# The first tile behind an output norm taken in two halves of the tokens

## The chip, the cores and the metric

The kernel runs on one core of one Trainium2 chip. The metric is the device time of one execution, in microseconds; the kernel before has a median of 3034.61 us over three runs (3032.1 to 3035.51).

## What is computed

Two blocks of a small language model, one sequence of 512 tokens, width 1024, all in float32. The second block has two layers. Each adds to x the output of a mixer (compressed, selected and windowed attention beside a stick-breaking attention) and then that of a feed-forward net with a depthwise convolution, and both outputs pass a norm of their own before they are added:

```python
x = x + rms_norm_2(mixer(rms_norm_2(x, g_pre_mix)), g_post_mix)
x = x + rms_norm_2(ffn(rms_norm_2(x, g_pre_ffn)), g_post_ffn)
# rms_norm_2(y, g) = y * rsqrt(mean(y * y, over the 1024 channels) + 1e-6) * g
```

The norms with g_post_mix and g_post_ffn are the output norms. There are four of them, two in each layer: ("p", 0, "m"), ("p", 0, "f"), ("p", 1, "m") and ("p", 1, "f") in the code.

## The kernel before

All activations lie transposed: channels on the 128 partitions, the 512 tokens along the free axis, so that x is eight tiles of 128x512, `K.x(0)` to `K.x(7)`. A product with a weight matrix is made in three passes of fp32r, each of 512 columns: high weights by high x and low weights by high x (`high`, lines 473 and 476), then high weights by low x (`low`, line 480). Weights stream from HBM through a ring. ScalarE rounds each piece of 512 columns (four 128x128 blocks) to the high part (line 996), VectorE subtracts it for the low part `wl` (line 1377); four pieces of each are held. Likewise ScalarE makes `xh(j)`, x times the gain of the next norm, rounded (`prescale`, line 1003), and VectorE the remainder `xl(j)` (line 1385). The factor of a pre-norm, one number for each token, is applied to the results only, so products start before the norm's sum is known.

The engines each run a program written out by hand, in order, and meet at semaphores: `q.wait_ge(flag, event)` is the wait, `tell` names the event.

An output norm can't be postponed in this way, since x + norm(y) is needed for the next product. Its steps:

- `post` on each engine. For each tile of y that TensorE ends, ScalarE squares it out of its bank (line 1007), VectorE adds the squares up and copies y to M (line 1787).
- TensorE: `sums` (lines 570 and 575) takes the column sums over the partitions, four products with a column of ones against the squares of tiles 0 to 6 and four against those of tile 7. The result is 128 tokens by 4 in bank 2.
- VectorE: `mean_square` (line 1399), on 128x4. GpSimd: `root` (line 1990), the power -1/2, on 128x4.
- TensorE: `spread` (line 585), four products with the identity, lays the roots as a row over all partitions, in bank 3.
- VectorE: `post_feed`, for each tile j: M times the gain times bank 3 (line 1797), x plus M (line 1800), and for the tile before, the remainder xl (line 1385).
- ScalarE: `post_feed`, for each tile j: xh(j) (line 1003) and the square of x(j) for the next norm (line 1007). GpSimd adds these squares up (`add_squares`, line 2024), one 128x512 addition for each of tiles 1 to 7.
- TensorE: `group`, five output tiles in five banks side by side, for k = 0 to 7: ten high passes with xh(k), then five low passes with xl(k).

On VectorE the feeds of tiles 0 to 2 come first; then, for each k, the feed of tile k + 3 and the low parts of the weight pieces up to the third beyond those of k. The group takes 40 blocks, that is pieces 0 to 9. The block of k = 6 and the third bank is the first of piece 8.

Behind three of the output norms a group follows. Behind the last one there is a tail (line 1975 on): VectorE makes M(0) to M(7) (line 1975) and adds x(0), x(2), x(4), x(6) (line 1979) and x(7) (line 1981), GpSimd adds x(1), x(3), x(5) (line 2064), and SyncE sends the eight tiles out in order.

`K.RSB` ("rs") is a row in SBUF. For pre-norms ScalarE copies the spread roots into it (`rs_row`, line 1011); output norms read them from bank 3.

Of the kernel before, what the change touches and what calls it, by code (L numbers as in the profile page):

```python
# [16 lines left out]
S = 512  # L17
# [21 lines left out]
for _name, _n in (("ident", 128), ("ones", 128), ("tri", 128), ("neg", 128), ("rot", 128), ("blk", 2), ("mhalf", 64),  # L39
# [6 lines left out]
         "x0", "first", "x1", "x2", "x3", "x4", "gain", "cst", "vec", "pos", "dil", "ret", "out")  # L46

# [398 lines left out]
def tensor_program(e, q, K):  # L446
# [72 lines left out]
    def group(key, nk, operand, banks, hooks):  # L519

        for k in range(nk):
            oh, parts = operand[0](k), []
# [90 lines left out]
    half = [None]  # L613

    def soft(L, steps, fill, upto):
# [3 lines left out]
        for t in range(n + 3):  # L619
# [28 lines left out]
            if 0 <= t - 3 < n:  # L648
                step = steps[t - 3]
                q.wait_ge(F.act, half[0])  # L650
# [14 lines left out]
                m.then_inc(F.attn.tell(("values", L, t - 3)), 1)  # L665
                if step.done is not None:
                    half[0] = step.done
# [47 lines left out]
    half[0] = "qkrow"  # L715
    vacated[4] = []
    soft(("e", 0), even_steps(K), fill, fill_even)
    vacated[4] = [(F.act, half[0])]
# [23 lines left out]
    def ffn(f, late):  # L742
        s = ("f", f)
        turn[0] = [0, 1, 4, 5, 6, 7]
        group(("up", f, "g"), DT, xn(s), [next_bank() for _ in range(5)], {} if late else norm(s))
# [5 lines left out]
    def post(s):  # L751

        sums(s, 6 % 3, apart=7 % 3)
        spread(s, 64, 3, F.dve, ("added", s))
# [65 lines left out]
    for l in range(2):  # L820
# [11 lines left out]
        group(("n", l, "g"), DT, xn(s), [next_bank() for _ in range(5)], {} if l else norm(s))  # L832
# [68 lines left out]
        half[0] = ("kcc", l)  # L901
# [31 lines left out]
        def sb_pv(n):  # L933
# [4 lines left out]
            if kt == 3:  # L938
                q.wait_ge(F.act, half[0])
# [3 lines left out]
            if kt == 0 and kv == 1:  # L943
                half[0] = ("os", l, j)
# [14 lines left out]
        vacated[4] = [(F.act, half[0])]  # L959
# [20 lines left out]
def scalar_program(e, q, K):  # L980
# [278 lines left out]
    def post_feed(s):  # L1259
        def feed(j):  # L1260
            q.wait_ge(F.dve, ("x", s, j))
            prescale(s, j)
# [5 lines left out]
    for l in range(2):  # L1268
        s = ("n", l)
        group(("n", l, "g"), 5, post_feed(s) if l else nothing, {} if l else {3: lambda: rs_row(s)})  # L1270
# [91 lines left out]
        ffn(2 + l, True, post_feed(("f", 2 + l)))  # L1362
        post(("p", l, "f"), ("down", 2 + l))


def vector_program(e, q, K):
# [315 lines left out]
    def rotate(h, which):  # L1682
# [10 lines left out]
        for i, (half, c) in enumerate(((0, K.cosr), (1, K.sinr), (0, K.sinr), (1, K.cosr))):  # L1693
# [3 lines left out]
            e.tensor_tensor(K.tmp(i), K.bank(keys[half])[:, :], c, ALU.mult).then_inc(F.dve.tell(*events), 1)  # L1697
# [82 lines left out]
    def post(s, key, M):  # L1780
# [191 lines left out]
    q.wait_ge(F.stat, ("spread", s))  # L1972
    q.wait_ge(F.dve, ("freed", "down", 3, DT - 1))
# [10 lines left out]
def gpsimd_program(e, q, K):  # L1984
    F = K.F
    def root(s, at, width=NQ):
# [4 lines left out]
            F.pool.tell(("rsn", s)), 1)  # L1991

# [35 lines left out]
    for l in range(2):  # L2028
# [28 lines left out]
        root(("p", l, "m"), 64)  # L2057
# [3 lines left out]
        root(("p", l, "f"), 64)  # L2061
# [163 lines left out]
```

## Time and profile before

| | |
|---|---|
| median of three runs | 3034.61 us (3032.1 to 3035.51) |
| the profiled execution, its own time | 3034.25 us |
| its span, first to last instruction | 3032.5 us |
| PE busy | 2998.2 us, 99% |
| DVE busy | 1774.3 us, 59% |
| ACT busy | 1269.7 us, 42% |
| POOL busy | 146.0 us, 5% |
| mean granted TensorE clock | 0.992 |

The span is shorter than the execution's own time by 1.75 us that lie around it. Engines are named as in the profile: PE is TensorE, DVE is VectorE, ACT is ScalarE, POOL is GpSimd. "L1797" is line 1797 of the kernel before. The granted clock is 1.00 at 2.4 GHz and 0.50 at 1.2 GHz. In the chain of waits and in the timeline a row with "x8" stands for eight records; one float32 product leaves two.

### The profile page before, as it was taken

What the parts mean: (1) busy time and instruction counts of PE and PEld (TensorE: products, weight loads), DVE (VectorE), ACT (ScalarE), POOL (GpSimd) and SP (SyncE); (2) the same over time, 40 slices, a digit from 0 to 9 for tenths busy, and PEclk for the clock granted to TensorE, in tenths of its full rate; (3) what the DMA queues carried; (4) which work ended last, traced back from release to release, by engine and by line L of the source; (5) the groups of instructions that cost most, each with busy time, mean ns of one, the idle gap of its engine ahead of it and who ended that gap; (6) DMA issues with size and microseconds to landing.
All of it is one profiled execution on the core that took longest, in us unless ns stands there. A gap on an engine that the chain in (4) does not pass through costs nothing.

```text
span 3032.5 us, 37840 instructions
## 1 busy us (share of the span) xinstructions
PE 2998.2 (99%) x14648; PEld 2400.0 (79%) x14648; DVE 1774.3 (59%) x3128; ACT 1269.7 (42%) x2377; POOL 146.0 (5%) x203
## 2 busy tenths in 40 slices
PE   9999999999999999999999999999999999999998
PEld 7778888877888888888876678888787766788886
DVE  4666775345555577634465557775364655577743
ACT  4444443322333344432366545443233655355431
POOL 0000000000000000001001101000020011010000
PEclk9999999999999999999999999999999999999999
DMA  4222322222222333333211132222232111223332
GB/s 156 71 94 94 99 97 97 98 77 84 84 77 88 93 98 97 98 97 98 92 36 43 48 99 80 101 97 98 84 102 88 36 42 49 90 84 105 98 97 70
DMA packets 72035, 260.35 MB, mean 86 GB/s; under 512 B 8112, under 2 KB 8112, under 8 KB 71728
## 3 DMA queue, kind: packets, MB, share of 16 engines
q1 hardware_dynamic: 70992, 254.52, 26.3%
q10 hardware_dynamic: 864, 3.41, 0.3%
q8 instruction: 116, 1.90, 0.3%
q14 instruction: 63, 0.52, 0.1%
HBM read 255.81 MB, written 2.10 MB: 85 GB/s over the span
## 4 chain that ended last, share of the span: by engine, by line
PE 93%; DVE 4%; ACT 2%; issue 1%; DMA 0%; POOL 0%; DVEq 0%; SPq 0%; ACTq 0%
PE bank L473 25%; PE bank L476 24%; PE bank L480 24%; PE bank L550 2%; PE bank L554 2%; PE bank L551 2%; PE bank L630 2%; PE bank L662 2%; PE bank L644 1%; PE bank L793 1%; PE bank L910 1%; DVE wl L1377 1%; DVE big L1961 1%; PE bank L940 1%; ACT big L1356 1%
## 5 line engine op out<-in xcount | busy, mean ns | idle before, releaser
L1377 DVE TENSOR_TENSOR wl<-ring,wh 128x512 fp32r<-128x512 f32 (+1 forms) x946 | 648.9, 692 | 829.2 <-ACT wh L996 824.4
L473 PE MATMUL bank<-xh,wh 128*128 128x512 f32 x2464 | 989.0, 401 | 14.1 <-ACT wh L996 7.2
L476 PE MATMUL bank<-xh,wl 128*128 128x512 f32 x2464 | 966.4, 392 | 0.3 <-DVE wl L1377 0.3
L480 PE MATMUL bank<-xl,wh 128*128 128x512 f32 x2464 | 926.2, 391 | 0.0
L996 ACT ACTIVATE wh<-ring 128x512 fp32r<-128x512 f32 (+1 forms) x946 | 581.0, 622 | 814.3 <-PE bank L480 734.7
L473 PEld LDWEIGHTS bank<-xh,wh 128*128 128x128 f32 x2464 | 466.3, 189 | 148.9 <-issue 38.4
L480 PEld LDWEIGHTS bank<-xl,wh 128*128 128x128 f32 x2464 | 465.1, 189 | 99.9 <-DVE xl L1470 0.4
L476 PEld LDWEIGHTS bank<-xh,wl 128*128 128x128 f32 x2464 | 466.9, 189 | 91.7 <-DVE wl L1377 1.3
L473 PE MATMUL bank<-bigr,wh 128*128 128x512 f32 x1024 | 399.0, 390 | 0.6 <-ACT bigr L1360 0.6
L476 PE MATMUL bank<-bigr,wl 128*128 128x512 f32 x1024 | 398.5, 389 | 0.0
L480 PE MATMUL bank<-bigr,wh 128*128 128x512 f32 x1024 | 393.4, 389 | 0.0
L473 PEld LDWEIGHTS bank<-bigr,wh 128*128 128x128 f32 x1024 | 192.2, 188 | 41.3 <-ACT bigr L1360 1.4
L480 PEld LDWEIGHTS bank<-bigr,wh 128*128 128x128 f32 x1024 | 192.2, 188 | 40.6 <-DVE bigr L1965 0.9
L476 PEld LDWEIGHTS bank<-bigr,wl 128*128 128x128 f32 x1024 | 192.2, 188 | 39.9
L1173 ACT ACTIVATE tmp<-tmp,vec 128x512 f32<-128x512 f32 x136 | 104.8, 770 | 182.1 <-DVE tmp L1427 182.1
L1065 ACT ACTIVATE pp<-pp,sm 128x512 f32<-128x512 f32 (+3 forms) x160 | 88.3, 553 | 90.7 <-DVE sm L1446 90.5
L1183 ACT ACTIVATE bigr<-tmp 128x512 fp32r<-128x512 f32 x88 | 55.6, 632 | 138.5 <-DVE tmp L1633 138.5
L1427 DVE TENSOR_TENSOR big<-bank,rs 128x512 f32<-128x512 f32 x106 | 71.7, 687 | 68.5 <-PE bank L480 65.4
L1990 POOL TENSOR_TENSOR sm<-sm,cst 128x4 f32<-128x4 f32 x16 | 16.6, 1037 | 1941.1 <-DVE sm L1399 1607.0
L1427 DVE TENSOR_TENSOR tmp<-bank,rs 128x512 f32<-128x512 f32 x154 | 105.4, 684 | 6.0 <-ACT rs L1011 4.3
L550 PE MATMUL bank<-wh,xh 128*128 128x512 f32 (+1 forms) x288 | 106.8, 371 | 0.0
L554 PE MATMUL bank<-wl,xh 128*128 128x512 f32 (+1 forms) x288 | 105.8, 367 | 0.0
(203 smaller groups left out, 2756.5 us busy)
## 6 DMA issues: line engine op xcount, KB each, us to landing
ring<-in_w_up SPq DMA_DIRECT2D x176, 512.0 KB, 3.5
ring<-in_w_down SPq DMA_DIRECT2D x88, 512.0 KB, 3.4
ring<-in_w_in SPq DMA_DIRECT2D x64, 512.0 KB, 3.5
ring<-in_w_ret SPq DMA_DIRECT2D x32, 512.0 KB, 3.3
ring<-in_w_even SPq DMA_DIRECT2D x19, 512.0 KB, 3.3
ring<-in_w_ret_v SPq DMA_DIRECT2D x16, 512.0 KB, 3.3
ring<-in_w_ret_out SPq DMA_DIRECT2D x16, 512.0 KB, 3.3
ring<-in_w_proj SPq DMA_DIRECT2D x16, 512.0 KB, 3.5
```

Of the source, the lines that this page charges most:

```text
L473: e.matmul(o, K.wh(p, c * 128, 128), oh, start=start, stop=False, skip_group_check=True)
L476: e.matmul(o, K.wl(p, c * 128, 128), oh, start=False, stop=False, skip_group_check=True)
L480: m = e.matmul(o, K.wh(p, c * 128, 128), ol, start=False, stop=stop, skip_group_check=True)
L550: e.matmul(o, K.XH[:, c], K.wh(p, 0, n), start=k == 0, stop=False)
L551: e.matmul(o, K.XL[:, c], K.wh(p, 0, n), start=False, stop=False)
L554: m = e.matmul(o, K.XH[:, c], K.wl(p, 0, n), start=False, stop=k == DT - 1)
L630: m = e.matmul(BK[i][:, u.at:u.at + w], u.q[r, u.qt * 128:w], u.k[r, 0:w], start=True, stop=True, skip_group_check=True)
L996: e.activation(K.wh(i, 0, w), K.raw(i), ACT.Copy, bias=0.0, scale=1.0).then_inc(F.hi.tell(("piece", i)), 1)
L1065: e.activation(p, p, ACT.Exp, bias=K.den(t, 2 * part + i, 0), scale=-1.0, accum_out=K.den(t, 2 * part + i, 1)).then_inc(F.act.tell(("exp", ...
L1173: e.activation(K.tmp((2 * i + 1) % 5), K.up(i), ACT.Identity, bias=b, scale=w[2]).then_inc(F.act.tell(("tap", f, i)), 1)
L1377: e.tensor_tensor(K.wl(i, 0, w), K.raw(i), K.wh(i, 0, w).bitcast(F32), ALU.subtract).then_inc(F.lo.tell(("piece", i)), 1)
L1427: e.tensor_tensor(dst, K.bank(key)[:, :], K.RSB[:, :], ALU.mult).then_inc(F.dve.tell(("freed", *key), *events), 1)
```

## The change

Each output norm is taken by halves of 256 tokens. Half 0 lies in bank 2 and half 1 in bank 3, from the sums to the spread roots. The sums, the mean squares (now two instructions of 128x2), the roots (two of 128x2) and the spreading tell an event for each half. The first tile of x is scaled, added and rounded to xh(0) in two halves, and in the group behind the norm the ten high passes of k = 0 become twenty of 256 columns: ten on half 0, then ten on half 1. ScalarE copies each half of the spread roots to `K.RSB`, behind VectorE's own reading of that half (`half_row`), and tiles 1 to 7 are scaled with `K.RSB` in SBUF where they were scaled with bank 3 in PSUM. The tail does so too, with tile 0 scaled in halves and then added whole. `half(ap, a)` is columns a * 256 to a * 256 + 255; the variable `half` of the tensor program is renamed `held`.

```diff
 tensor_program, group (called with border=True for the groups behind an output norm)
+            if border and k == 0:
+                s = ("f", key[1]) if key[0] == "up" else key[:2]
+                for a in range(2):
+                    q.wait_ge(F.act, ("xh", s, 0, a))
+                    for m, b in enumerate(banks):
+                        if a == 0:
+                            empty(b)
+                            K.place[(*key, m)] = b
+                            vacated[b] = [(F.dve, ("freed", *key, m))]
+                            parts.append(take())
+                        high(half(BK[b], a), *parts[m], half(K.xh(0), a), a == 0)
+                ol = operand[1](k)
+                for m, b in enumerate(banks):
+                    low(BK[b][:, :], *parts[m], ol, False)
+                continue
 tensor_program, post
-        sums(s, 6 % 3, apart=7 % 3)
-        spread(s, 64, 3, F.dve, ("added", s))
+        q.wait_ge(F.dve, ("sq", s))
+        empty(2)
+        empty(3)
+        for i in range(NQ):
+            e.matmul(BK[2 + i // 2][:, i:i + 1], K.tmp(6 % 3)[:, i * 128:(i + 1) * 128], K.cs("ones", 1), start=i % 2 == 0,
+                     stop=False, skip_group_check=True)
+        q.wait_ge(F.act, ("sq", s, DT - 1))
+        for i in range(NQ):
+            m = e.matmul(BK[2 + i // 2][:, i:i + 1], K.tmp(7 % 3)[:, i * 128:(i + 1) * 128], K.cs("ones", 1), start=False,
+                         stop=i % 2 == 1, skip_group_check=True)
+            if i % 2:
+                m.then_inc(F.stat.tell(("sums", s, i // 2)), 1)
+        for i in range(NQ):
+            if i % 2 == 0:
+                q.wait_ge(F.pool, ("rsn", s, i // 2))
+            m = e.matmul(BK[2 + i // 2][:, i * 128:(i + 1) * 128], bc(K.SM[:, 64 + i:65 + i], [[0, 128]]), K.cs("ident"),
+                         start=True, stop=True, skip_group_check=True)
+            if i % 2:
+                m.then_inc(F.stat.tell(("spread", s, i // 2)), 1)
+        vacated[2] = vacated[3] = [(F.act, ("rs", s))]
 scalar_program
+    def half_row(s, a):
+        q.wait_ge(F.stat, ("spread", s, a))
+        q.wait_ge(F.dve, ("m", s, 0, a))
+        e.activation(half(K.RSB, a), half(BK[2 + a], a), ACT.Copy, bias=0.0, scale=1.0).then_inc(
+            F.act.tell(("rsh", s, a), *([("rs", s)] if a else [])), 1)
 scalar_program, post_feed
-            q.wait_ge(F.dve, ("x", s, j))
-            prescale(s, j)
+            if j == 0:
+                for a in range(2):
+                    half_row(before, a)
+                    q.wait_ge(F.dve, ("x", s, 0, a))
+                    e.activation(half(K.xh(0), a), half(K.x(0), a), ACT.Copy, bias=0.0,
+                                 scale=K.vec(GAIN[s][0], GAIN[s][1])).then_inc(
+                        F.act.tell(("xh", s, 0, a), *([("xh", s, 0)] if a else [])), 1)
+            else:
+                q.wait_ge(F.dve, ("x", s, j))
+                prescale(s, j)
 vector_program, post
-        mean_square(s, DT * 128)
+        for a in range(2):
+            q.wait_ge(F.stat, ("sums", s, a))
+            e.tensor_scalar(K.SM[:, 2 * a:2 * a + 2], BK[2 + a][:, 2 * a:2 * a + 2], 1.0 / (DT * 128), EPS, ALU.mult,
+                            ALU.add).then_inc(F.dve.tell(("ms", s, a)), 1)
+    def half_scale(s, key, M, gain, a):
+        q.wait_ge(F.stat, ("spread", s, a))
+        q.wait_ge(F.dve, ("freed", *key, DT - 1))
+        e.scalar_tensor_tensor(out=half(M[0], a), in0=half(M[0], a), scalar=gain, in1=half(BK[2 + a], a), op0=ALU.mult,
+                               op1=ALU.mult).then_inc(F.dve.tell(("m", s, 0, a), *([("m", s, 0)] if a else [])), 1)
 vector_program, post_feed
-            q.wait_ge(F.stat, ("spread", s))
             if j == 0:
-                q.wait_ge(F.dve, ("freed", *key, DT - 1))
-            e.scalar_tensor_tensor(out=M[j], in0=M[j], scalar=K.vec(gain, gi + j), in1=BK[3][:, :], op0=ALU.mult,
-                                   op1=ALU.mult).then_inc(F.dve.tell(("m", s, j), *([("added", s)] if j == DT - 1 else [])), 1)
-            q.wait_ge(F.dve, ("m", s, j))
-            e.tensor_tensor(K.x(j), K.x(j), M[j], ALU.add).then_inc(F.dve.tell(("x", nxt, j)), 1)
+                for a in range(2):
+                    half_scale(s, key, M, K.vec(gain, gi), a)
+                    q.wait_ge(F.dve, ("m", s, 0, a))
+                    e.tensor_tensor(half(K.x(0), a), half(K.x(0), a), half(M[0], a), ALU.add).then_inc(
+                        F.dve.tell(("x", nxt, 0, a)), 1)
+            else:
+                q.wait_ge(F.act, ("rs", s))
+                e.scalar_tensor_tensor(out=M[j], in0=M[j], scalar=K.vec(gain, gi + j), in1=K.RSB[:, :], op0=ALU.mult,
+                                       op1=ALU.mult).then_inc(F.dve.tell(("m", s, j)), 1)
+                q.wait_ge(F.dve, ("m", s, j))
+                e.tensor_tensor(K.x(j), K.x(j), M[j], ALU.add).then_inc(F.dve.tell(("x", nxt, j)), 1)
 vector_program, the tail behind the last output norm
     for j in range(DT):
-        e.scalar_tensor_tensor(out=XM[j], in0=XM[j], scalar=K.vec("g_post_ffn_2", 8 + j), in1=BK[3][:, :], op0=ALU.mult,
-                               op1=ALU.mult).then_inc(F.dve.tell(("m", s, j)), 1)
+        if j == 0:
+            for a in range(2):
+                half_scale(s, ("down", 3), XM, K.vec("g_post_ffn_2", 8), a)
+        else:
+            q.wait_ge(F.act, ("rs", s))
+            e.scalar_tensor_tensor(out=XM[j], in0=XM[j], scalar=K.vec("g_post_ffn_2", 8 + j), in1=K.RSB[:, :], op0=ALU.mult,
+                                   op1=ALU.mult).then_inc(F.dve.tell(("m", s, j)), 1)
 gpsimd_program
+    def half_roots(s):
+        for a in range(2):
+            q.wait_ge(F.dve, ("ms", s, a))
+            e.tensor_tensor(K.SM[:, 64 + 2 * a:66 + 2 * a], K.SM[:, 2 * a:2 * a + 2], K.cs("mhalf", 2), ALU.pow).then_inc(
+                F.pool.tell(("rsn", s, a)), 1)
```

## Rows read from the trace of the kernel before

**Rows 1.** Page, part 4: the chain that ended last, share of the span by engine

```profile
PE 93%; DVE 4%; ACT 2%; issue 1%; DMA 0%; POOL 0%; DVEq 0%; SPq 0%; ACTq 0%
```

**Rows 2.** Chain of waits after the output norm at 1816 us: start us, us, what

```profile
1817.21 0.97 PE bank L575 x8
1818.20 0.17 DVE sm L1399
1818.44 1.02 POOL sm L1990
1819.51 1.17 PE bank L585 x8
1820.70 0.76 DVE big L1797
1821.48 0.70 DVE x L1800
1822.21 0.73 ACT xh L1003
1822.98 0.79 PE bank L473
```

**Rows 3.** The spreading in the chain at the third and the fourth output norm

```profile
2647.04 2.09 PE bank L585 x8
3019.49 2.09 PE bank L585 x8
```

**Rows 4.** Stretches: length, busy of PE, PEld, DVE, ACT, POOL, granted clock, DMA, GB/s

```profile
1822.98:1852.63 29.65, 29.65 (x121) 24.37 (x122) 24.14 (x31) 15.07 (x25) 10.02 (x7) 0.92 0.26 88
2194.08:2224.21 30.13, 30.13 (x121) 24.71 (x122) 24.39 (x31) 14.85 (x25) 9.81 (x7) 0.91 0.30 87
2651.43:2681.55 30.12, 30.12 (x121) 24.70 (x122) 24.39 (x31) 14.92 (x25) 9.82 (x7) 0.91 0.28 84
```

**Rows 5.** Chain of waits: full products at each clock, a product of 256 columns

```profile
1823.77 0.43 PE bank L476
1829.06 0.23 PE bank L476
1638.22 0.12 PE bank L927
```

**Rows 6.** Groups by form, small shapes: busy us, mean ns of one, idle before

```profile
L1997 POOL TENSOR_TENSOR sm<-sm,cst 128x64 f32<-128x64 f32 x1 | 10.6, 10642 | 41.6 <-DVE sm L1522 41.6
L1941 DVE TENSOR_TENSOR tmpr<-pp,bigr 128x256 fp32r<-128x256 f32 x16 | 6.0, 418 | 0.0
```

**Rows 7.** Timeline: start us, us, engine; VectorE and GpSimd in the first group

```profile
1824.91 1.83 POOL L2024 TENSOR_TENSOR tmp<-tmp 128x512 f32<-128x512 f32 x1 [5.46 <-ACT tmp L1007]
1825.52 1.77 DVE L1385 SCALAR_TENSOR_TENSOR xl<-x,vec,xh 128x512 fp32r<-128x512 f32 x1
...
1833.76 0.73 DVE L1797 SCALAR_TENSOR_TENSOR big<-big,vec,bank 128x512 f32<-128x512 f32 x1
1834.53 1.25 DVE L1800 TENSOR_TENSOR x<-x,big 128x512 f32<-128x512 f32 x1
1835.70 0.74 DVE L1385 SCALAR_TENSOR_TENSOR xl<-x,vec,xh 128x512 fp32r<-128x512 f32 x1
1833.93 1.30 POOL L2024 TENSOR_TENSOR tmp<-tmp 128x512 f32<-128x512 f32 x1 [1.91 <-ACT tmp L1007]
```

**Rows 8.** The late weight remainders (timeline), and their product (chain of waits)

```profile
1844.19 2.99 DVE L1377 TENSOR_TENSOR wl<-ring,wh 128x512 fp32r<-128x512 f32 x3
...
1846.97 0.23 PE bank L476
```

**Rows 9.** Timeline of the tail, VectorE and GpSimd

```profile
3021.61 1.41 DVE L1975 SCALAR_TENSOR_TENSOR xm<-xm,vec,bank 128x512 f32<-128x512 f32 x2 [3.25 <-PE bank L585]
3029.29 0.68 DVE L1981 TENSOR_TENSOR x<-x,xm 128x512 f32<-128x512 f32 x1
3023.09 1.65 POOL L2064 TENSOR_TENSOR x<-x,xm 128x512 f32<-128x512 f32 x1 [3.65 <-DVE xm L1975]
```

More of the change, by code:

```diff
@@ L46, with half @@
          "x0", "first", "x1", "x2", "x3", "x4", "gain", "cst", "vec", "pos", "dil", "ret", "out")
+def half(ap, a):
+    return ap[:, a * S // 2:(a + 1) * S // 2]
 class Flag:
@@ L517, in tile, with group @@
             pass
-    def group(key, nk, operand, banks, hooks):
+    def group(key, nk, operand, banks, hooks, border=False):
         for k in range(nk):
-            oh, parts = operand[0](k), []
+            parts = []
+            if border and k == 0:
[13 more added lines that the diff above has]
+                continue
+            oh = operand[0](k)
             for m, b in enumerate(banks):
@@ L611, in fills @@
         return fill
-    half = [None]
+    held = [None]
     def soft(L, steps, fill, upto):
@@ L649, in soft @@
                 step = steps[t - 3]
-                q.wait_ge(F.act, half[0])
+                q.wait_ge(F.act, held[0])
                 if step.cmp is not None:
@@ L666, in soft @@
                 if step.done is not None:
-                    half[0] = step.done
+                    held[0] = step.done
     def cmp_turn(l, j):
@@ L712, in tensor_program @@
         vacated[b] = [(F.dve, ("qk", j))]
-    half[0] = "qkrow"
+    held[0] = "qkrow"
     vacated[4] = []
     soft(("e", 0), even_steps(K), fill, fill_even)
-    vacated[4] = [(F.act, half[0])]
+    vacated[4] = [(F.act, held[0])]
     def mixed(k):
@@ L744, in ffn @@
         turn[0] = [0, 1, 4, 5, 6, 7]
-        group(("up", f, "g"), DT, xn(s), [next_bank() for _ in range(5)], {} if late else norm(s))
+        group(("up", f, "g"), DT, xn(s), [next_bank() for _ in range(5)], {} if late else norm(s), late)
         for i in range(5, 2 * FT):
@@ L831, in tensor_program @@
         turn[0] = [0, 1, 4, 5, 6, 7]
-        group(("n", l, "g"), DT, xn(s), [next_bank() for _ in range(5)], {} if l else norm(s))
+        group(("n", l, "g"), DT, xn(s), [next_bank() for _ in range(5)], {} if l else norm(s), l == 1)
         tile(("n", l, 5), DT, xn(s), F.dve, norm(s, 0, 4) if l else {})
@@ L900, in tensor_program @@
         fill = fills(steps(("gm", l, j), DT, xn(s), F.dve) for j in range(16))
-        half[0] = ("kcc", l)
+        held[0] = ("kcc", l)
         soft(("n", l), nsa_steps(K, l), fill, fill_nsa)
@@ L938, in sb_pv @@
             if kt == 3:
-                q.wait_ge(F.act, half[0])
+                q.wait_ge(F.act, held[0])
             e.matmul(BK[4][base:base + 64, kt * 128:S], K.SBV[:, kt * S + h * 64:kt * S + (h + 1) * 64],
@@ L943, in sb_pv @@
             if kt == 0 and kv == 1:
-                half[0] = ("os", l, j)
+                held[0] = ("os", l, j)
         for t in range(16 + 2):
@@ L958, in tensor_program @@
         fill(10 ** 6)
-        vacated[4] = [(F.act, half[0])]
+        vacated[4] = [(F.act, held[0])]
         def merged(k):
@@ L1257, in post, with post_feed @@
             square(s, j, K.bank((*key, j))[:, :])
-    def post_feed(s):
-        def feed(j):
-            q.wait_ge(F.dve, ("x", s, j))
-            prescale(s, j)
+    def half_row(s, a):
[3 more added lines that the diff above has]
+            F.act.tell(("rsh", s, a), *([("rs", s)] if a else [])), 1)
+    def post_feed(s, before):
+        def feed(j):
+            if j == 0:
[8 more added lines that the diff above has]
+                prescale(s, j)
             if j >= 3:
@@ L1269, in scalar_program @@
         s = ("n", l)
-        group(("n", l, "g"), 5, post_feed(s) if l else nothing, {} if l else {3: lambda: rs_row(s)})
+        group(("n", l, "g"), 5, post_feed(s, ("p", 0, "f")) if l else nothing,
+              {} if l else {3: lambda: rs_row(s)})
         if l:
@@ L1361, in scalar_program @@
         post(("p", l, "m"), ("wo", l))
-        ffn(2 + l, True, post_feed(("f", 2 + l)))
+        ffn(2 + l, True, post_feed(("f", 2 + l), ("p", l, "m")))
         post(("p", l, "f"), ("down", 2 + l))
+    for a in range(2):
+        half_row(("p", 1, "f"), a)
 def vector_program(e, q, K):
@@ L1692, in rotate @@
                 q.wait_ge(F.act, ("oh", 4 * h - 5))
-        for i, (half, c) in enumerate(((0, K.cosr), (1, K.sinr), (0, K.sinr), (1, K.cosr))):
+        for i, (part, c) in enumerate(((0, K.cosr), (1, K.sinr), (0, K.sinr), (1, K.cosr))):
             events = [("rt", h, which, i)]
@@ L1696, in rotate @@
                 events += [("freed", *key) for key in keys]
-            e.tensor_tensor(K.tmp(i), K.bank(keys[half])[:, :], c, ALU.mult).then_inc(F.dve.tell(*events), 1)
+            e.tensor_tensor(K.tmp(i), K.bank(keys[part])[:, :], c, ALU.mult).then_inc(F.dve.tell(*events), 1)
     def centre(h):
@@ L1971, in vector_program @@
     s = ("p", 1, "f")
-    q.wait_ge(F.stat, ("spread", s))
-    q.wait_ge(F.dve, ("freed", "down", 3, DT - 1))
     for j in range(DT):
-        e.scalar_tensor_tensor(out=XM[j], in0=XM[j], scalar=K.vec("g_post_ffn_2", 8 + j), in1=BK[3][:, :], op0=ALU.mult,
-                               op1=ALU.mult).then_inc(F.dve.tell(("m", s, j)), 1)
+        if j == 0:
[5 more added lines that the diff above has]
+                                   op1=ALU.mult).then_inc(F.dve.tell(("m", s, j)), 1)
         if j % 2:
@@ L1991, in root @@
             F.pool.tell(("rsn", s)), 1)
+    def half_roots(s):
+        for a in range(2):
+            q.wait_ge(F.dve, ("ms", s, a))
+            e.tensor_tensor(K.SM[:, 64 + 2 * a:66 + 2 * a], K.SM[:, 2 * a:2 * a + 2], K.cs("mhalf", 2), ALU.pow).then_inc(
+                F.pool.tell(("rsn", s, a)), 1)
     s = ("e",)
@@ L2056, in gpsimd_program @@
                                     channel_multiplier=-1).then_inc(F.pool.tell(("w", l, n)), 1)
-        root(("p", l, "m"), 64)
+        half_roots(("p", l, "m"))
         for j in range(DT):
@@ L2060, in gpsimd_program @@
         root(("f", 2 + l), 224)
-        root(("p", l, "f"), 64)
+        half_roots(("p", l, "f"))
     for j in (1, 3, 5):
```

## The prediction

> **What bounds the kernel now.** I read the page's chain first: TensorE holds 93% of it, VectorE 4%, ScalarE 2% [rows 1]. So only two things count, the places where TensorE stands still and the stretches in which its clock is low. The output norms are such places. The chain of waits in the window of the first one shows a relay with one engine working at a time [rows 2]: last sums 0.97, mean 0.17, root 1.02, spreading 1.17, scaling 0.76, addition 0.70, xh(0) 0.73, then the first product at 1822.98. From 1817.21 that is 5.77 us without a product of weights. The second norm has the same relay. At the third and the fourth the spreading takes 2.09 [rows 3], 0.92 more, because the clock is already at its lower level (1.2 GHz).
>
> The clock stays low behind the gap. A product of 512 columns takes 0.43 there and 0.23 at full clock [rows 5]. From restart to the end of the group the mean granted clock is 0.92, 0.91 and 0.91 [rows 4]; at two levels, 1.00 and 0.50, that is 2 x 0.08 x 29.65 = 4.7 us low, then 5.4 and 5.4.
>
> Then I looked at what feeds the group. In the timeline one feed of VectorE is scaling (L1797), addition (L1800), remainder (L1385) and one weight remainder (L1377). An operation starts 0.07 to 0.08 before the one ahead of it has ended: two scalings take 1.41 in all [rows 9], so 0.67 each from start to start, and an addition 0.61. The four would be 0.67 + 0.61 + 0.67 + 0.61 = 2.55, but the addition takes 1.25, because GpSimd began its own addition (1.30) at 1833.93 [rows 7]. So a feed costs about 3.2 against 15 x 0.227 = 3.4 of TensorE for one k. VectorE keeps ahead, but narrowly: the first of three late weight remainders, piece 8, ends at 1844.19 + 2.99 - 2 x 0.61 = 1845.96, and the product that needs it starts at 1846.97 [rows 8]. The lead is 1.0 us.
>
> **The relay by halves.** Times are of the first norm. Half 0 of the sums is done after four of eight records, 0.48 sooner, at 1817.70; VectorE's copy of the last tile stands in front of the mean, so I take 1817.75, and 1817.99 for the start of the root. GpSimd's power takes 1.02 on four columns [rows 2] and 10.64 on 64 [rows 6], 0.16 for each column, so 0.70 on two (bounds 0.51, half, and 1.02, nothing gained). Half 0 has its roots at 1818.69, half 1 at 1819.39. Spreading one half is half of 1.17: half 0 is out at 1819.31, half 1 at 1820.02. An operation of 256 columns on VectorE takes 0.42 [rows 6], a scaling 0.05 more as at 512. VectorE then does scaling, addition, scaling, addition: 1819.34, 1819.83, 1820.17, 1820.66, and is free for tile 1 at 1821.10, where it was at 1821.48 + 0.61 = 1822.09: 1.0 us sooner. ScalarE first copies half of the row (new, some 0.37, done at 1820.20 while the addition runs), then xh(0), half 0, at 1820.27: between 0.37 and 0.73, taken as 0.50. TensorE restarts at 1820.82, 2.15 sooner (1.6 to 2.5). Half 1 is rounded at 1821.65, when the first ten short products still run until about 1823.1; there is no new wait there. Behind ScalarE's new waits stand only its own feeds of tiles 1 and 2, which VectorE feeds later anyway.
>
> Twenty products of 256 columns replace ten of 512: 0.12 against half of 0.227 [rows 5], 0.1 more in all at full clock, 0 to 0.5 at the low one. Unhindered, TensorE would be 2.0 us ahead.
>
> **What takes this back.** Tiles 1 to 7 are now scaled with a row in SBUF. The scaling beside GpSimd's addition took 0.73, undisturbed, as its row lay in a bank; an operation of the same kind with both tensors in SBUF, L1385, took 1.77 behind GpSimd's 1.83, and ended 0.55 behind it [rows 7]. So two engines take turns: an operation of VectorE with two SBUF tensors doesn't run beside GpSimd's addition, in either order. The Trainium skill, page "SBUF — State Buffer", section "SBUF: two separate sides", has this as an exclusive lock for the whole instruction between a GpSimd operation and a VectorE one with two SBUF inputs; taken alone it gives 1.29 for each of GpSimd's additions, in the groups and three times in the tail. The rows price it so: GpSimd asked 0.17 behind the start of the scaling; now it must let the scaling end, 0.50 later, and everything behind it moves by that. A feed costs 3.2 + 0.5 = 3.7, more than TensorE's 3.4. VectorE becomes the bound of the group.
>
> In place of the bank's slot a scaling of its own costs the same, 0.73 against 0.74 [rows 7]. The Trainium skill, page "VectorE: DVE Perf Modes", section on the TRN2 errata, gives 58 cycles of fixed cost from SBUF and 120 from PSUM; at 0.96 GHz that would save 0.065 for each of 28 scalings, 1.8 us in all and 3031.8 us. The trace doesn't agree, and I leave it out.
>
> Piece 8 again. VectorE starts tile 1 1.0 sooner and loses 0.5 of it while the first two additions of GpSimd are placed; the three feeds from tile 4 to tile 7 cost 0.53 more each, 1.6; and GpSimd's last addition, which stood in front of the subtraction (2.99 for three [rows 8]), comes a little later than it, so 1.0 to 1.2 is saved. Sum: -0.5 + 1.6 - 1.0 = +0.1; piece 8 is ready at 1846.1. TensorE, 2.0 ahead, would want it at 1845.0, and waits 1.1. From this product to the end of the stretch there are 1852.63 - 1846.97 = 5.66. Because of the wait a clock that rises up to 2 us later costs nothing.
>
> - Group 1 ends at 1846.1 + 5.66 = 1851.8 instead of 1852.63: -0.85.
> - Group 2: restart was 371.10 later [rows 4], so 2217.2 + 5.66 = 2222.9 instead of 2224.21: -1.35.
> - Group 3: 828.45 later, less the 0.92 of slow spreading, of which half 0 pays 0.4: 2674.0 + 5.66 = 2679.7 instead of 2681.55: -1.85.
>
> Together -4.1. Bounds: -7.0, with the feeds as cheap as before, and +1.
>
> **The tail.** Here the relay matters less, since the next row copy needs half 1. The first scaling was at 3021.61, 0.92 of slow spreading included. Now half 0 is spread at 3019.8, half 1 at 3020.9; scaling and copy end at 3021.75, and tile 1 is scaled at 3021.77 instead of 3021.61 + 0.67 = 3022.28: -0.5. But GpSimd adds three tiles, 1.65 each, beside scalings from the bank [rows 9]. Now nothing of VectorE's seven scalings and five additions can run beside them. Each addition of 1.29 stops VectorE for 1.2: +3.6 (between 0, if they run beside after all, and 3 x 1.65 = 4.9). VectorE's last addition, which ended at 3029.97, ends at about 3033.1. The outputs follow as before. Tail: +3.1. Should VectorE win each turn, GpSimd's three would be left for the end, at the same price.
>
> **Sum.** 3034.25, the profiled execution's own time, - 4.1 + 3.1 = 3033.25. That execution lies 0.36 under the median, so 3033.6 for a median. SyncE's weight loads depend on pieces used and start up to 2 us earlier or not at all; each lands in its slot well ahead, and I cost them at nothing.
>
> **Rivals.**
> - A, the scaling from SBUF does run beside GpSimd. For it: nothing but that this very operation isn't in the trace. Then groups gain 2.0, 2.0 and 2.3, the tail 0.5: 3027.8. Chance 0.07.
> - B, GpSimd is served ahead of VectorE at the end of the feeds too, so that its last addition still stands before piece 8. The place is the product of 1846.97; it decides once the remainder is written later than that. Piece 8 is then ready at 1847.3 to 1847.8, groups end +0.6, +0.1 and -0.4 or 0.5 worse, tail +3.1 to +3.6: 3038.5. For it: GpSimd was ahead there before the change (three subtractions took 2.99, undisturbed they take 1.91) [rows 8]. Chance 0.2, a quarter of it beyond 0.2%, where ScalarE's later rounding adds to it.
> - C, the lower clock lasts one stretch longer in a group, as at the third norm where it fell earlier: up to 1.7 for each beyond the cover of the wait: 3035.5. Chance 0.13.
> - My case, 0.6.
>
> A measurement of this kernel can tell 0.2%, 6.1 us, from no change. A lies just beyond it; faster gets 0.06, slower 0.07, the rest 0.87. The range reaches from most of A's side, 3029.8, to B, 3038.8.
>
> **What would show it.** Right: the relay's first product some 2.1 us sooner; rows of L1797's successor with a mean well over 0.74 and up to 1.9; a wait of TensorE of 0.5 to 1.7 on wl at k = 6 in each group; the tail's VectorE stretched by 3 to 4 us. Wrong: scalings at 0.74 beside GpSimd (A), no wait on wl while the groups end 2 us sooner, or waits of over 2 us in several k.

## The result, and the profile of the changed kernel

The changed kernel takes 3038.77 us (median of 20 runs, 3032.91 to 3040.84), the kernel before 3033.65 beside it (20 runs, 3029.07 to 3035.93). The ratio is 1.0016, 95% interval 1.0010 to 1.0022: slower by 5 us, where I had forecast 3033.6 and no difference. The profiled execution took 3038.75, its span 3036.9, which is 4.4 over the span before.

The page, part 4, shows the chain by engine; it answers to [rows 1]:

```profile
PE 90%; DVE 7%; ACT 2%; issue 1%; POOL 0%; ACTq 0%; DVEq 0%
```

TensorE holds 90% of the chain instead of 93%, VectorE 7% instead of 4%. What TensorE waits for, by the waits of PE (engine, line waited for: us in total, times, longest us):

```profile
PE bank L481 <- DVE wl L1435: 7.4, 6, 2.2
PE bank L478 <- ACT wh L1036: 6.9, 3, 6.2
PE bank L790 <- POOL sm L2073: 2.3, 4, 0.6
PE bank L478 <- ACT xh L1312: 2.2, 3, 0.9
```

The last two are the shortened relay: they come to 4.5, and the same two waits of the kernel before to 7.0 + 5.4. The first one is new. Before, waits on weight remainders came to 0.3 us in the whole kernel.

**The relay** of the first norm in the chain of waits, which answers to [rows 2]:

```profile
1817.00 0.69 DVE big L1845
1817.69 0.14 DVE sm L1849
1817.84 0.07 issue
1817.91 0.70 POOL sm L2073
1818.61 0.04 issue
1818.66 0.73 PE bank L790 x4
1819.38 0.02 issue
1819.41 0.49 DVE big L1856
```

and the restart in the timeline of TensorE (start us, us, engine, what, idle before and what ended it):

```profile
1820.94 0.58 PE L478 MATMUL bank<-xh,wh 128*128 128x256 f32 x1 [0.91 <-ACT xh L1312]
1821.32 0.42 PE L481 MATMUL bank<-xh,wl 128*128 128x256 f32 x1
1821.53 0.42 PE L478 MATMUL bank<-xh,wh 128*128 128x256 f32 x1
```

VectorE copies the last tile of y at 1817.00 (1817.09 before). The first product follows at 1820.94, 3.94 later; before it was 5.89. The root of two columns took the 0.70 I had worked out. At the low clock a short product starts 0.21 after the one ahead, half of the 0.43 in [rows 5].

**The groups**, by windows, with the columns of [rows 4], from the first product to the last low pass of k = 7:

```profile
1820.94:1855.09 34.15, 31.34 (x131) 25.78 (x132) 28.13 (x33) 15.33 (x27) 10.97 (x7) 0.90 0.23 77
2194.57:2227.39 32.82, 30.54 (x131) 25.39 (x132) 28.39 (x34) 15.56 (x27) 10.97 (x7) 0.92 0.25 80
2651.45:2684.01 32.56, 30.45 (x131) 25.62 (x132) 28.16 (x33) 15.46 (x27) 10.69 (x7) 0.91 0.25 79
```

The groups are 4.5, 2.7 and 2.4 us longer than in [rows 4], together 9.6; the relay gave 2.0, 1.9 and 2.9, together 6.8. Length less busy is what TensorE stood still: 2.81 (two waits, 0.66 and 2.15), 2.28 and 2.11, nothing before. The rest is busier time, 92.3 for the three instead of 89.9.

**Where TensorE stands still.** One feed, and the end of the feeds, in the timeline of VectorE and GpSimd; they answer to [rows 7, 8]:

```profile
1834.54 0.75 DVE L1870 SCALAR_TENSOR_TENSOR big<-big,vec,rs 128x512 f32<-128x512 f32 x1
1834.71 1.72 POOL L2107 TENSOR_TENSOR tmp<-tmp 128x512 f32<-128x512 f32 x1 [3.90 <-ACT tmp L1047]
1835.32 1.66 DVE L1873 TENSOR_TENSOR x<-x,big 128x512 f32<-128x512 f32 x1
...
1845.60 1.30 POOL L2107 TENSOR_TENSOR tmp<-tmp 128x512 f32<-128x512 f32 x1 [1.91 <-ACT tmp L1047]
1845.70 2.96 DVE L1435 TENSOR_TENSOR wl<-ring,wh 128x512 fp32r<-128x512 f32 x3
```

GpSimd asks at 1834.71, again 0.17 behind the start of the scaling, and now ends 1.72 later, not 1.30. VectorE's addition stretches from 1.25 to 1.66. The last two rows are the point: GpSimd's last addition starts 0.10 ahead of the three late subtractions, so piece 8 again waits for it. In the kernel before, GpSimd stood ahead of the subtractions of 1844.19 [rows 8] by the same 0.10:

```profile
1844.09 1.34 POOL L2024 TENSOR_TENSOR tmp<-tmp 128x512 f32<-128x512 f32 x1 [2.46 <-ACT tmp L1007]
```

The chain of waits at the same place in the changed kernel:

```profile
1845.78 1.68 DVE wl L1435
1847.46 0.04 issue
1847.50 0.50 PE bank L481
1848.00 0.23 PE bank L478
1848.23 0.34 PE bank L481
1848.57 0.43 PE bank L478
1849.00 0.43 PE bank L481
1849.42 2.13 PE bank L485 x5
1851.56 0.33 PE bank L478
```

TensorE stood still for 2.15 us until 1847.50, worked for 0.7 us at full clock, and fell to 1.2 GHz (0.43 a product) until 1851.6. In the second and third group the waits at this place were 2.17 and 2.11, and the clock stayed up.

**The tail**, VectorE and GpSimd in the timeline, which answers to [rows 9]:

```profile
3023.62 0.75 DVE L2051 SCALAR_TENSOR_TENSOR xm<-xm,vec,rs 128x512 f32<-128x512 f32 x1 [0.51 <-ACT rs L1303]
...
3024.45 1.64 POOL L2147 TENSOR_TENSOR x<-x,xm 128x512 f32<-128x512 f32 x1 [2.65 <-DVE xm L2051]
3024.89 2.41 DVE L2051 SCALAR_TENSOR_TENSOR xm<-xm,vec,rs 128x512 f32<-128x512 f32 x2
...
3033.69 0.68 DVE L2057 TENSOR_TENSOR x<-x,xm 128x512 f32<-128x512 f32 x1
```

Each of three pairs of scalings takes 2.40, where a pair took 1.41. From the copy of the last tile (3019.53, before 3017.08) to the end of the last addition it is 14.84 instead of 12.89.

**The account.** The time from the copy of the last tile to the first product falls from 18.60 to 11.84 for the three norms: -6.8. The groups grow by 7.2 of standing still and 2.4 of busier time: +9.6. The tail grows by 1.95. Together +4.8, beside a span that grew by 4.4. The relay worked, and the groups gave back more than it brought.

### The profile page after: what moved, and what is told of

The parts are those of the page before. It is cut to its first block, busy times and chain, and to the rows that moved or that the text cites. A ratio compares the mean times of both kernels' runs of the same rounds, so it can differ in the third digit from the quotient of the medians.

```text
span 3036.9 us, 37934 instructions
## 1 busy us (share of the span) xinstructions
PE 3000.1 (99%) x14678; PEld 2403.9 (79%) x14678; DVE 1787.1 (59%) x3139; ACT 1272.2 (42%) x2388; POOL 150.3 (5%) x207
## 4 chain that ended last, share of the span: by engine, by line
PE 90%; DVE 7%; ACT 2%; issue 1%; POOL 0%; ACTq 0%; DVEq 0%
PE bank L478 24%; PE bank L485 24%; PE bank L481 24%; PE bank L572 2%; PE bank L576 2%; PE bank L573 2%; PE bank L652 2%; PE bank L684 2%; PE bank L666 1%; DVE wl L1435 1%; PE bank L833 1%; PE bank L950 1%; DVE x L1873 1%; DVE big L2034 1%; PE bank L980 1%
## 5 line engine op out<-in xcount | busy, mean ns | idle before, releaser
L478 PE MATMUL bank<-xh,wh 128*128 128x512 f32 (+1 forms) x2479 | 993.3, 401 | 9.1 <-ACT wh L1036 6.9
L481 PE MATMUL bank<-xh,wl 128*128 128x512 f32 (+1 forms) x2479 | 971.2, 392 | 7.5 <-DVE wl L1435 7.4
L573 PE MATMUL bank<-wh,xl 128*128 128x512 f32 (+1 forms) x288 | 105.9, 368 | 0.0
```

Source lines behind the costliest of these rows:

```text
L478: e.matmul(o, K.wh(p, c * 128, 128), oh, start=start, stop=False, skip_group_check=True)
L481: e.matmul(o, K.wl(p, c * 128, 128), oh, start=False, stop=False, skip_group_check=True)
L573: e.matmul(o, K.XL[:, c], K.wh(p, 0, n), start=False, stop=False)
```

## The experiments

Each ran in five rounds beside the kernel before, whose median was 3033.8 beside the first seven (28 runs at first, then 19) and 3032.97 beside the last two. My theory after the result: (1) a scaling with its row in SBUF takes turns with GpSimd's additions, which makes the feeds 0.4 us longer and the tail 3; (2) with the feeds late, GpSimd's last addition in front of piece 8 decides, as rival B had it. Rivals were that the short products or the longer way over ScalarE cost the time, or that the clock alone made the difference. The diffs show the lines that matter; `...` stands for the rest.

**The row in SBUF alone**, without halves:

```diff
-        spread(s, 64, 3, F.dve, ("added", s))
+        spread(s, 64, 3, F.act, ("rs", s))
 scalar_program
+    def row(before):
+        q.wait_ge(F.stat, ("spread", before))
+        q.wait_ge(F.dve, ("m", before, 0))
+        e.activation(K.RSB[:, :], BK[3][:, :], ACT.Copy, bias=0.0, scale=1.0).then_inc(F.act.tell(("rs", before)), 1)
...
 vector_program, post_feed and tail
+    q.wait_ge(F.act, ("rs", s))
-    in1=BK[3][:, :]
+    in1=K.RSB[:, :] if j else BK[3][:, :]
...
```

> The kernel before, with one part of the change alone: ScalarE copies the spread roots to a row in SBUF once VectorE has scaled tile 0 from the bank, and tiles 1 to 7 are scaled with that row (in the tail too). No halves. Theory (a scaling with its row in SBUF can't run beside GpSimd's additions, so VectorE falls behind and piece 8 of the weight remainders is late): a feed costs 3.6 us where it cost 3.2, TensorE waits 0.5 to 1.7 us for piece 8 in each of the three groups, 3.4 in all, and the tail's three additions of GpSimd stop VectorE for 1.0 each, 3.0. Time 3040 us against 3033.7 before. Rival (the halves are what costs: twenty short products for ten, more small instructions, ScalarE's copies in front of xh(0)): no wait for piece 8, feeds of 3.2, tail as before; 3034.

Measured: 3040.15 us (11 runs), ratio 1.0021, interval 1.0012 to 1.0030. TensorE waits on weight remainders for 4.9 us, 1.7 at most, at the places of the changed kernel; a pair of scalings in the tail takes 2.40. So the row's place, with ScalarE's copy that puts it there, makes the kernel slower without any halves, by 6.4 us where the whole change costs 5.1. The halves are not what cost. That it is the place and not the copy, the next run shows: it keeps the copies and the halves.

**GpSimd's additions cut to one column.** This kernel leaves out all but the first column of GpSimd's sums of squares, and divides by 128 where these sums are used, so its time is that of a kernel without that load:

```diff
-            e.tensor_tensor(K.tmp(j % 3), K.tmp(j % 3), K.tmp((j - 1) % 3), ALU.add).then_inc(
+            e.tensor_tensor(K.tmp(j % 3)[:, 0:1], K.tmp(j % 3)[:, 0:1], K.tmp((j - 1) % 3)[:, 0:1], ALU.add).then_inc(
...
```

> The changed kernel, but GpSimd's additions of the squares in the groups behind output norms take one column of 512, so they hold the shared port for next to nothing; the sums of squares of those three pre-norms then lack tiles 0 to 6 in all columns but one (the divisor is 128 in place of 1024 to keep sizes alike). The tail is left as changed. Theory: feeds of 2.6 us, no wait for piece 8, the groups keep the 2 us that the halves bring at each of three norms, the tail still loses 1.9: 3029 to 3030 us. Rival (halves cost): nothing changes at all, 3038.8.

Measured: 3025.60 us (9 runs), ratio 0.9976, interval 0.9967 to 0.9986. Groups by line, VectorE, in the first group (busy us, mean ns, idle before):

```profile
L1870 DVE SCALAR_TENSOR_TENSOR big<-big,vec,rs 128x512 f32<-128x512 f32 x7 | 5.2, 746 | 0.1
L1873 DVE TENSOR_TENSOR x<-x,big 128x512 f32<-128x512 f32 x7 | 4.8, 692 | 0.2
```

VectorE's additions are back at 692 ns from 1.66 us, and no wait on a weight remainder is left in the groups. Everything the groups lost hangs on GpSimd's additions. It came out some 4 us better than I expected. The table below shows 2.2 of that as less busy time of TensorE in the groups than in the kernel before, where I had counted on none; the rest lies outside the places in the table.

**Piece 8 ahead of GpSimd.** One line in the changed kernel's `post_feed` of VectorE, behind the addition of tile 7:

```diff
                 e.tensor_tensor(K.x(j), K.x(j), M[j], ALU.add).then_inc(F.dve.tell(("x", nxt, j)), 1)
+            if j == DT - 1:
+                lo_to(K.W.first[("up", nxt[1], "g") if nxt[0] == "f" else (*nxt, "g")] + 8)
             if j:
                 prescale(nxt, j - 1)
```

> The changed kernel; VectorE subtracts piece 8 between the addition of tile 7 and the remainder of tile 6, in place of behind both remainders, where GpSimd's last addition got in first. Theory: piece 8 is ready 2.5 us earlier, the wait of 2.1 to 2.2 us in each group goes, and with it the low clock that followed it in the first group; a wait of some tenths may appear at piece 7 or at xl(6) instead. 3032 to 3033 us. Rival (TensorE's waits are covered by the low clock, or move whole to the next operand, xh(7) or xl(6)): less than 1.5 gained, 3037.5 or more.

Measured: 3029.47 us (11 runs), ratio 0.9984, interval 0.9975 to 0.9993. The timeline of the first group, VectorE and GpSimd:

```profile
1841.06 1.67 DVE L1873 TENSOR_TENSOR x<-x,big 128x512 f32<-128x512 f32 x1
1842.65 0.68 DVE L1435 TENSOR_TENSOR wl<-ring,wh 128x512 fp32r<-128x512 f32 x1
1843.25 1.41 DVE L1443 SCALAR_TENSOR_TENSOR xl<-x,vec,xh 128x512 fp32r<-128x512 f32 x2
1844.09 1.72 POOL L2109 TENSOR_TENSOR tmp<-tmp 128x512 f32<-128x512 f32 x1 [1.91 <-ACT tmp L1047]
```

The subtraction takes 0.68 and is done at 1843.33, 0.76 us before GpSimd's addition begins. The waits on weight remainders fall from 7.4 to 1.3, 0.4 at most. No work was taken away and none made shorter, and the kernel gains 9 us on the changed one. So the order at that one place is what the result turned on. The waits are 6.1 of it. Behind the norms and inside the groups the granted clock is low for 13.7 us in this trace and for 20.5 in that of the changed kernel; at half speed that is 3.4 us more. I had expected 3032 to 3033 us; I had counted on losing only the low stretch behind the wait in the first group, and twice as much low clock is gone.

**The row back in the bank**, with the halves kept. Half 1's bank gets the whole row, and ScalarE's copies go:

```diff
-            m = e.matmul(BK[2 + i // 2][:, i * 128:(i + 1) * 128], ...
+        for a in range(2):
+            q.wait_ge(F.pool, ("rsn", s, a))
+            for i in range(2 + 2 * a):
+                m = e.matmul(BK[2 + a][:, i * 128:(i + 1) * 128], ...
...
 vector_program, post_feed and tail
-    in1=K.RSB[:, :]
+    in1=BK[3][:, :]
```

> The changed kernel with the row back in PSUM: half 0 of the roots is spread into bank 2 as in the change, and then all four columns into bank 3 (two products more), from which half 1 and tiles 1 to 7 are scaled; ScalarE's copies of the row go. Theory: feeds cost 3.2 again, no wait for piece 8, half 1 of tile 0 some 0.4 later, the tail loses nothing to GpSimd: three groups 1.7 to 2 us better than before, tail 0.5 better: 3027 to 3028 us. Rival (halves cost): about 3038, less the tail's 3.0, so 3036.

Measured: 3025.37 us (8 runs), ratio 0.9972, interval 0.9962 to 0.9983. One feed again, in the timeline:

```profile
1830.17 0.73 DVE L1866 SCALAR_TENSOR_TENSOR big<-big,vec,bank 128x512 f32<-128x512 f32 x1
1830.34 1.29 POOL L2102 TENSOR_TENSOR tmp<-tmp 128x512 f32<-128x512 f32 x1 [1.91 <-ACT tmp L1047]
1830.94 1.24 DVE L1869 TENSOR_TENSOR x<-x,big 128x512 f32<-128x512 f32 x1
```

The rows of [rows 7] are back to the hundredth, and a feed is 3.20 from scaling to scaling. I had expected no wait for piece 8, and that was wrong: waits of 4.0 us on weight remainders are left, 1.2 to 1.3 at piece 8. With the restart 2 us earlier, a subtraction behind GpSimd's last addition is late for TensorE even so. The time is 2 us below what I expected all the same; in this trace the clock is low for 6.8 us behind the norms and in the groups, 20.5 in that of the changed kernel.

**Both, row in the bank and piece 8 early:**

> The kernel with the full row spread into the bank again (run e4_bank_row), and piece 8 of each group subtracted between the addition of tile 7 and the remainder of tile 6, as in e3_piece8_early. Theory (what is left of waits in e4_bank_row is GpSimd's last addition standing before piece 8): the wait of 1.2 us at piece 8 goes in each of the three groups and no more than 0.4 us at one place is left; time 2 to 3.5 us below e4_bank_row's 3025.4, so near 3022.5. Rival (the wait moves on to the next operand of the group by as much): waits of 4 us in all as before, time 3025 or more.

Measured: 3021.27 us (6 runs), ratio 0.9964, interval 0.9952 to 0.9976. The wait on weight remainders:

```profile
PE bank L481 <- DVE wl L1432: 0.3, 2, 0.2
```

The theory held, with 4.1 us where I had said 2 to 3.5. This kernel beats both the one before, by 12.5 us, and the changed one.

**The tail alone undone**: in the changed kernel the last norm's whole row goes to bank 3, and the tail scales from there.

```diff
-        for i in range(NQ):
-            if i % 2 == 0:
-                q.wait_ge(F.pool, ("rsn", s, i // 2))
+        last = s == ("p", 1, "f")
+        for a in range(2):
+            q.wait_ge(F.pool, ("rsn", s, a))
+            for i in range(0 if last else 2 * a, 2 + 2 * a):
...
 vector_program, tail
-            in1=K.RSB[:, :]
+            in1=BK[3][:, :]
```

> The changed kernel with one thing undone: behind the last norm the full row is spread into a bank and the last output tiles are scaled from there, not from the SBUF row; the three groups keep the SBUF row. Theory: pairs of scalings in the tail take 1.40 again and not 2.40, three of them, so the time is 3.0 us below the changed kernel's 3038.8: 3035.7 (3035.3 to 3036.1). Rival (the tail ends on the transfer out or on GpSimd's additions and the scalings are covered): no change, 3038.8.

Measured: 3035.25 us (11 runs), ratio 1.0005, interval 0.9996 to 1.0014; 3.5 below the changed kernel. In the timeline of the tail:

```profile
3018.41 1.65 POOL L2144 TENSOR_TENSOR x<-x,xm 128x512 f32<-128x512 f32 x1 [2.47 <-DVE xm L2048]
3018.85 1.40 DVE L2048 SCALAR_TENSOR_TENSOR xm<-xm,vec,bank 128x512 f32<-128x512 f32 x2
```

The pairs take 1.40 beside the same 1.65 of GpSimd. The tail's part of the loss is shown by itself.

**Full products again**, with the row in the bank: the group's first piece in products of 512 columns, which wait for both halves of the tile.

```diff
-        group(("up", f, "g"), DT, xn(s), [next_bank() for _ in range(5)], {} if late else norm(s), late)
+        group(("up", f, "g"), DT, xn(s), [next_bank() for _ in range(5)], {} if late else norm(s))
...
```

> e4_bank_row with the group's first piece in full products of 512 columns, so that TensorE waits for both halves of the first tile. Theory (what the halves buy is the earlier restart, and what the start buys is partly eaten by the wait at piece 8): restart 0.7 to 0.9 us later in each group, of which the wait at piece 8 takes up most; time 1 us over e4_bank_row's 3025.4, between 3025.4 and 3028. Rival (the longer gap lets the clock fall once more): a stretch of 3.4 us or more at the low clock behind the second norm, which e4_bank_row has not, and 3028 to 3030.

Measured: 3025.38 us (8 runs), ratio 0.9975, interval 0.9965 to 0.9985. The restarts are 1.1 to 1.5 us later, the waits on weight remainders fall from 4.0 to 1.2, and the time is that of e4_bank_row, where I had expected 1 us more. In the table below the longer gaps (+3.8) and the shorter waits (-3.3) nearly cancel: an earlier restart bought next to nothing while piece 8 was late. The trace also has what the rival named, 6.8 us of low clock behind the second norm, where e4_bank_row has none, without the longer time that the rival went with.

**Piece 8 early in the kernel before**, and **full products with piece 8 early**; the edits are the ones above.

> The kernel before with one line added: piece 8 of each group is subtracted ahead of the remainder of tile 6, so ahead of GpSimd's last addition; no halves. Theory (the relay by halves is worth its 2 us a group once nothing in the group is late): the waits on weight remainders in the kernel before are 0.3 us in all, so the new place has nothing to give: 3033.8, within 1 us, and the run with the bank's row, the halves and piece 8 early (3021.3) stands some 12 us below it. Rival (the new place is worth something by itself, as the three late subtractions hold up more than piece 8): 3030 or less.

Measured: 3033.53 us (11 runs), ratio 1.0003, interval 0.9994 to 1.0012. The new place gives nothing where piece 8 isn't late, as the theory had it. In its trace the granted clock falls ahead of the first norm's spreading, which takes 2.09 us, where in that of the kernel before it falls behind it (1.17), although the two run the same code up to there.

> e5_bank_early with the group's first piece in full products of 512 columns, as e7_bank_full_products is to e4_bank_row. There the later restart was paid out of the wait at piece 8, and the time stayed at 3025.4. Theory: without that wait nothing takes it up, and 1.1 us in each of three groups show: 3021.3 + 3.3 = 3024.6 (3023.5 to 3026). Rival (the short products cost as much as their earlier start gives): 3021.3 within 1 us.

Measured: 3022.87 us (5 runs), ratio 0.9967, interval 0.9955 to 0.9980. That is 1.6 above e5_bank_early, half of what I expected; by the intervals of the two the measurement can't tell them apart. In the trace of e5_bank_early the second group, at full clock, takes 28.22, and here it takes 27.53. The short products cost 0.12 of that (k = 0 takes 3.86 and 3.74). The rest, 0.5, lies at k = 1 and 2, whose low passes are 3.54 and 3.78 behind those of the k ahead, where the pitch is 3.40. TensorE has caught up with VectorE's feeds there: in the first group of e5_bank_early the chain of waits runs over VectorE's scalings, additions and remainders up to the product at 1828.77. So of the 1.1 that the short products start earlier, some 0.4 to 0.5 is left for a group. The windows of the three groups here:

```profile
1816.68:1844.22 27.54, 27.54 (x121) 22.79 (x122) 24.25 (x32) 14.63 (x25) 10.61 (x7) 1.00 0.28 89
...
2638.26:2667.35 29.09, 29.09 (x121) 23.98 (x122) 24.23 (x32) 15.30 (x25) 10.58 (x7) 0.94 0.27 89
```

A group without a wait and without the low clock takes 27.54. In the kernel before, with 29.65 to 30.13 [rows 4], 2.1 to 2.6 us of each group were the clock's.

All of them in one table, in us. Gap is the time from the copy of the last tile to the first product, for three norms; busy and still are TensorE's in the three groups; the tail is from the last copy to the end of the last addition; low is the time that the trace shows at 1.2 GHz in the stretches that begin behind one of the first three norms or in their groups. All but the first column come from one profiled execution each.

| kernel | median | gap | busy | still | tail | sum | low |
|---|---|---|---|---|---|---|---|
| before | 3033.65 | 18.6 | 89.9 | 0.0 | 12.9 | 121.4 | 23.9 |
| changed | 3038.77 | 11.8 | 92.3 | 7.2 | 14.8 | 126.2 | 20.5 |
| e1 row in SBUF only | 3040.15 | 19.2 | 89.2 | 4.6 | 16.8 | 129.7 | 23.9 |
| e2 one-column additions | 3025.60 | 12.9 | 87.7 | 0.0 | 14.8 | 115.3 | 17.1 |
| e3 piece 8 early | 3029.47 | 12.3 | 88.6 | 1.0 | 14.8 | 116.7 | 13.7 |
| e4 row in bank | 3025.37 | 12.4 | 86.6 | 4.2 | 12.0 | 115.1 | 6.8 |
| e5 bank, piece 8 early | 3021.27 | 12.4 | 85.4 | 0.3 | 11.6 | 109.7 | 6.8 |
| e6 tail from bank | 3035.25 | 11.9 | 92.4 | 6.7 | 11.6 | 122.6 | 20.5 |
| e7 bank, full products | 3025.38 | 16.2 | 86.4 | 0.9 | 11.6 | 115.1 | 13.7 |
| e8 before, piece 8 early | 3033.53 | 20.5 | 89.4 | 0.0 | 12.9 | 122.8 | 30.7 |
| e9 e5, full products | 3022.87 | 16.0 | 84.2 | 0.0 | 11.6 | 111.7 | 6.8 |

The sums follow the medians within 2.2 us, so these places hold the difference between the kernels. What the sums leave out are mainly stretches of low clock at 35 and 97 us, which come and go from trace to trace in kernels that are the same up to there (the profiled execution of e6_bank_tail has neither, and its span, 3027.8, is far below its median).

## Why the prediction was wrong, step by step

- **The relay: right.** I had 2.15 us, from 5.89 to 3.94 it was 1.95, and 2.9 at the third norm, where the granted clock is still 1.00 while half 0 is spread (0.73 us at 2649.17). Root, spreading, scaling, addition and copy came within about 0.1 of the steps.
- **Short products: right** at 0.1 us for ten of them (0.12 in e5_bank_early against e9_early_full), and nothing more at the low clock.
- **The turns between VectorE and GpSimd: right**, against rival A. A feed went from 3.2 to 3.63; I had 3.7. The Trainium skill, page "SBUF — State Buffer", section "SBUF: two separate sides", has GpSimd and a VectorE operation with two SBUF inputs exclude each other for the whole instruction; the runs agree, as a GpSimd addition that starts during a scaling takes 1.72 with the row in SBUF and 1.29 with it in the bank (e4_bank_row), and VectorE's addition behind it 1.66 and 1.24, but 0.69 where GpSimd adds one column. That a scaling would be cheaper from SBUF, by the Trainium skill, page "VectorE: DVE Perf Modes", section on the TRN2 errata, isn't borne out: 0.75 from SBUF, 0.73 from the bank, and 0.746 for seven of them where GpSimd adds one column.
- **The tail: right in mechanism, a little high in size.** Three pairs at +1.0 are 3.0, where I had 3.6; the earlier start gave 1.1 where I had 0.5. It came to +1.95, not +3.1; undoing it gave 3.5 by the medians.
- **Piece 8: the step that failed.** I wrote that "GpSimd's last addition, which stood in front of the subtraction (2.99 for three [rows 8]), comes a little later than it, so 1.0 to 1.2 is saved". It started 0.10 ahead of it, as before. I had moved the subtraction and the addition by separate reckonings, whose difference was smaller than the error of either. But the two are tied, since both go on from ScalarE's xh(7): behind it ScalarE squares the tile (0.62) and GpSimd may start, and behind it VectorE makes the remainder xl(7) (0.75) and comes to piece 8. A delay of the feeds shifts both alike, so the order at their end had to stay what it was in [rows 8]. Beside it two sizes were wrong that nearly cancel, which is luck. Up to tile 4 I allowed 0.5 for GpSimd's first additions: three of them stopped VectorE for 1.05 to 1.13 each (before 1.03 and 0.32), and tile 4 was scaled at 1831.89, against 1830.79 before, where I had 0.5 sooner. From tile 4 to tile 7 I had 1.6 more, and it was 0.54 (9.91 us, before 9.37). Piece 8 was ready at 1847.46, 1.5 later than before, where I had 0.1: 1.0 of the difference is the place in the order. So a wait of 1.1 became 2.1 to 2.2, three times.
- **The clock: missed.** I had it only as rival C, a stretch longer behind a norm, and covered by the wait. It fell instead behind the new wait in the first group, and e6_bank_tail shows the same fall. No later wait covers it there: of the 4.5 us by which this group is longer, 1.7 us are half of the 3.4 us at the low clock. At the restart the clock was low for 3.4 us of the group and not 4.7, which gave 0.6 back.
- **What could be told apart: too coarse.** I took anything under 0.2% for no change. The interval of the ratio reaches from 1.0010 to 1.0022, so 5 us the wrong way are clear of the noise.

In sum I had the groups, relay included, at -4.1 and got -6.76 + 9.63 = +2.9; that is the error, with the tail 1.1 the other way. It was rival B, to which I had given 0.2, and it had piece 8 right (1847.3 to 1847.8; measured 1847.46). That its price, 3038.5, is what was measured is partly luck: it had the tail at +3.1 to +3.6 where +1.95 was measured, and nothing for the fall of the clock in the first group. e3_piece8_early shows that this step alone carried the sign: with it mended, the changed kernel is faster than the one before.

What stays open is why the clock falls where it does. Two kernels with the same groups (changed and e6) show the same low stretches behind all three norms. But e4, e5 and e9 have a third of them, with gaps from 3.9 to 5.9 us that overlap those of the others, and in e9, with the longer gap, the clock stays up behind two norms. What e4, e5, e7 and e9 have in common is twelve records of spreading in the gap instead of eight. e7 has 13.7, so this doesn't settle it. Nor is one trace of each enough: the kernel before and e8 have the same relay and the same median, and their traces have 23.9 and 30.7 us. Of the 11.7 us by which the sum of e5_bank_early lies below that of the kernel before, 6.2 are the gaps, 1.3 the tail and 4.5 the busy time in the groups, less 0.3 of standing still. The clock gives more than these 4.5: it is low for 15.9 us of the three groups before and for 2.7 in e5, which is 6.6 at half speed, and the short products and the feeds at k = 1 and 2 take some 2 back. I can't say that the same would come of it in another kernel.

## What to carry to other kernels

Where two engines may not work side by side, ask at the end of a run of such work which of the two stands in front of the operand that is due next, and take the order from a chain of dependences rather than from a difference of two estimated times; put the due operand ahead of the other engine's turn. Keep an input that is read again and again beside GpSimd's work in a bank if one is free, and move it to SBUF only when the bank is needed. A shorter gap pays only as far as what feeds the engine behind it comes earlier too, so look for the first operand that would then be late.

## What the runs showed of the hardware that I had not expected

- GpSimd's power takes 0.70 on two columns, 1.02 on four [rows 2] and 10.64 on 64 [rows 6]: all three fit a fixed 0.4 and 0.16 for each column, an estimate from these rows. So splitting a small one costs 0.4 in all but brings its first half out 0.3 sooner.
- A wait of 2.15 us inside a group was followed by the low clock in two kernels (the changed one and e6_bank_tail, both in the first group), and waits of 2.17 and 2.11 in the other groups were not. Waits of up to 1.7 were followed by none.
- Gaps of 5.05 us behind the first two norms left the clock at 1.00 in e9_early_full, and gaps of 3.94 to 3.96 in the changed kernel did not.
